# An expert chosen in the last mixer block becomes job 0: its weights load over the mixer's weights, and its token list is made ahead of the job table

## What is computed

```python
h    = rms_norm(x, norm_mix)
proj = h @ w_in + b_in                       # gates and u of a short convolution | q, k, v
x    = x + concat(rms_norm(y_conv), rms_norm(y_attn)) @ w_out + b_out
h2   = rms_norm(x, norm_ffn)
logits = h2 @ w_router + b_router            # 32 experts
top_vals, top_idx = lax.top_k(logits, 4);  gates = softmax(top_vals)
# for each expert e, over the tokens that picked it:
hid = h2[toks] @ w1[e] + b1[e]               # w1[e] 1024 x 2048
y   = clamped_swiglu(hid) @ w2[e] + b2[e]    # w2[e] 1024 x 1024
x[toks] += gate * y
```

## Time and profile before

| | us |
|---|---|
| median of 3 runs | 1974.45 |
| lowest, highest | 1973.93, 1977.43 |
| span of the profiled execution | 1973.8 |
| mixer, start to the barrier's release | 0 to 461.95 |
| setup of the experts, to the first piece of job 0 | 461.95 to 490.11 |
| jobs, to the end | 490.11 to 1973.8 |
| PE busy | 1912.5 (97%) |
| DVE busy | 1302.9 (66%) |

### The profile page before, as it was taken

The page is one execution under the profiler, slowest core; times in us unless marked ns, Lnnn a source line. Parts: engine busy times, 40 slices in busy tenths (PEclk is TensorE's granted clock), DMA queues, the critical chain, the costliest instruction groups (busy, mean ns, idle before and its releaser), DMA issues.

```text
span 1973.8 us, 33290 instructions
## 1 busy us (share of the span) xinstructions
PE 1912.5 (97%) x12224; PEld 1390.5 (70%) x12224; DVE 1302.9 (66%) x3759; ACT 411.4 (21%) x910; POOL 238.3 (12%) x317
## 2 busy tenths in 40 slices
PE   7999999997999999999999999999899999999996
PEld 5677777774999999999999999833334444444442
DVE  2787778764376777776666666634537766777665
ACT  1233332222121122222222222222212100001100
POOL 1212222221010011111111111110100000000000
PEclk9999999998999999999999999999999999999998
DMA  9411100004966787788888989999999999999992
GB/s 310 113 43 43 43 22 31 32 33 150 340 208 218 248 271 258 245 282 282 283 287 294 307 295 310 312 377 373 358 379 384 358 361 354 368 369 367 361 360 71
DMA packets 207682, 498.39 MB, mean 253 GB/s; under 512 B 7716, under 2 KB 14928, under 8 KB 200080
## 3 DMA queue, kind: packets, MB, share of 16 engines
q1 hardware_dynamic: 194016, 449.43, 63.2%
q0 software_dynamic: 11312, 39.85, 8.2%
q10 hardware_dynamic: 2304, 8.39, 1.0%
HBM read 470.24 MB, written 27.41 MB: 252 GB/s over the span
## 4 chain that ended last, share of the span: by engine, by line
PE 39%; issue 35%; POOL 1%; DVE 1%; DMA 0%; POOLq 0%; ACT 0%; DVEq 0%; ACTq 0%
PE ps_unit L1886 38%; POOL x_got L1378 1%; DMA x_got<-h_rows,idx_next 0%; PE ps_list L1858 0%; POOL carrier L1374 0%; POOL out_dram L1435 0%; POOLq L1096 0%; DVE match L1562 0%; POOL out_dram L1390 0%; DVE reached L1610 0%; POOLq L1426 0%; POOLq L1265 0%; DVE xT L1684 0%; ACT xT L1466 0%; POOLq L1413 0%
## 5 line engine op out<-in xcount | busy, mean ns | idle before, releaser
L1886 PE MATMUL ps_unit<-xT,w_slot 128*128 128x136 f32 (+6 forms) x3840 | 521.5, 298 | 1.5 <-DVE xT L1684 1.5
L1886 PEld LDWEIGHTS ps_unit<-xT,w_slot 128*128 128x128 f32 x3840 | 516.6, 196 | 1.9 <-issue 1.9
L1916 PE MATMUL ps_unit<-w_slot,xT 128*128 128x512 f32 x704 | 306.7, 594 | 1.2 <-DVE xT L1279 1.2
L1279 DVE STREAM_TRANSPOSE xT<-x_got 32x256 f32<-32x256 f32 x644 | 280.5, 436 | 30.5 <-DMA x_got<-h_rows,idx_next 22.0
L1886 PE MATMUL ps_unit<-act_T,w_slot 128*128 128x136 f32 (+6 forms) x1920 | 261.6, 298 | 0.1
L1886 PEld LDWEIGHTS ps_unit<-act_T,w_slot 128*128 128x128 f32 x1920 | 257.9, 190 | 2.2 <-DVE act_T L1659 1.5
L1916 PEld LDWEIGHTS ps_unit<-w_slot,xT 128*128 128x128 f32 x704 | 132.8, 190 | 164.3 <-issue 164.3
L1675 DVE STREAM_TRANSPOSE y_rows<-yT 32x256 f32<-32x256 f32 x372 | 162.1, 436 | 55.0 <-ACT yT L1481 50.1
L928 PE MATMUL ps_c<-hT,w_in_sb 128*128 128x128 f32 x1536 | 182.0, 278 | 5.5 <-DMA w_in_sb<-in_w_in_dram 5.5
L928 PEld LDWEIGHTS ps_c<-hT,w_in_sb 128*128 128x128 f32 x1536 | 177.2, 194 | 10.7 <-DMA w_in_sb<-in_w_in_dram 6.3
L1374 POOL TENSOR_TENSOR carrier<-carrier 128x1 f32<-128x1 f32 x64 | 15.8, 247 | 1320.4 <-issue 610.7
(11 more groups left out here) (294 smaller groups left out, 1835.6 us busy)
## 6 DMA issues: line engine op xcount, KB each, us to landing
w_slot<-in_w_dram SPq DMA_DIRECT2D x192, 2048.0 KB, 11.1
b_row<-in_b_dram SPq DMA_DIRECT2D x11, 1024.0 KB, 12.9
w_in_sb<-in_w_in_dram SPq DMA_DIRECT2D x6, 1024.0 KB, 12.0
b_row<-in_b_dram SPq DMA_DIRECT2D x11, 512.0 KB, 15.1
x_in<-in_x_dram SPq DMA_DIRECT2D x8, 512.0 KB, 3.5
x_res<-in_x_dram SPq DMA_DIRECT2D x8, 512.0 KB, 4.8
out_dram<-x ACTq DMA_DIRECT2D x8, 512.0 KB, 5.3
h_rows<-h ACTq DMA_DIRECT2D x8, 512.0 KB, 3.3
```

The lines of the kernel that those rows point to most:

```text
L1279: last = nc.vector.transpose(out[c * Q:(c + 1) * Q, :, tokens], rows.rearrange("p (k c j) -> p k c j", c=P // Q, j=Q)[:, :, c, :])
L1886: last = pe.matmul(ps_unit[p % RING][:, u, 0:n], w, moving[:, k, 0:n], start=(k == 0), stop=(k == KD - 1))
L1916: last = pe.matmul(ps_hid[c], xT[:, k, 0:P], w_slot[:, c, k, :], start=(k == 0), stop=(k == KD - 1))
```

## The change

1. In the last block PE sums the picks of the first seven blocks (`ps_tally`), and DVE takes the expert with the most (`choose_first`): a copy, a max, its index and two casts into `first_e` and `first_i`. This stands between two conv steps of DVE and its wait for the attention scores.
2. The expert slots are no longer memory of their own: `w_slot` lies over the mixer's weights in one tensor `w_store`. In the last block SP loads job 0's first-layer weights after `conv_done[3]` and its second-layer weights after `attn_mixed`. POOL loads the bias rows after `attn_mixed`, into what was left of `w_store` and into `x_in`.
3. In the setup DVE first works out the places of the chosen expert's tokens alone, then its size class, and POOL splits that expert's gates. PE lists the tokens before it does anything for the table. `hold_clock(5)` at the start and eight `hold_clock` matmuls ahead of the jobs go; `hold_clock(6)` comes in ahead of `first_rows`.
4. DVE's work on the table follows after the list of job 0 is read. A new term `leads` of the order key puts the chosen expert first.
5. PE runs job 0 from a body of its own, one for each of the 12 sizes, found by a chain of compares. In it, the keys are spread after piece 0, the fields after piece 1, and the list of job 1 is made after piece 4 instead of 2. PE reads the counts of jobs only after job 0, and its loops start at job 1.
6. The copies `iota_b` and two fifths of `entry` move from ACT in the setup to DVE ahead of the first block.

```diff
+            sp.wait_ge(first_chosen, 1)
+            e = sp.value_load(first_i[0:1, 0:1], min_val=0, max_val=NE - 1)
+            wait(sp, conv_done[CC - 1], NB - 1)
+            for i in range(W1_LOADS):
+                load_pieces(sp, w_slot, w1, w2, w_loaded, i, e)
+            wait(sp, attn_mixed, NB - 1)
+            for i in range(W1_LOADS, LOADS):
+                load_pieces(sp, w_slot, w1, w2, w_loaded, i, e)
...
+                if not more:
+                    wait(pool, x_normed, t)
+                    wait(pool, attn_mixed, t)
+                    pool.dma_start(b1_rows[:, 0:D], b1[0, :, 0:D]).then_inc(pool_moved.sem, 16)
+                    pool.dma_start(b1_rows[:, D:2 * D], b1[0, :, D:2 * D]).then_inc(rows_moved.sem, 16)
+                    pool.dma_start(b2_rows, b2[0]).then_inc(pool_moved.sem, 16)
...
+            def choose_first():
+
+                dve.wait_ge(tallied, 1)
+                fstep.did(nc.vector.tensor_copy(tally[:], ps_tally))
+                dve.wait_ge(fstep.sem, fstep.n)
+                fstep.did(nc.vector.max(tally_top[:], tally[:]))
+                dve.wait_ge(fstep.sem, fstep.n)
+                fstep.did(nc.vector.max_index(tally_i[:], tally_top[:], tally[:]))
+                dve.wait_ge(fstep.sem, fstep.n)
+                fstep.did(nc.vector.tensor_copy(first_e[:], tally_i[:, 0:1]))
+                dve.wait_ge(fstep.sem, fstep.n)
+                nc.vector.tensor_copy(first_i[:], first_e[0:1, :]).then_inc(first_chosen, 1)
...
+                if not more:
+                    wait(pe, added_up, NB - 2)
+                    pe.matmul(ps_tally, ones_b[:], before[:, NB - 1, :], start=True, stop=True).then_inc(tallied, 1)
...
-            pool.dma_start(y_rows[0:NE, 0, :], b1[0, :, 0:D]).then_inc(pool_moved.sem, 16)
-            pool.dma_start(y_rows[0:NE, 1, :], b1[0, :, D:2 * D]).then_inc(rows_moved.sem, 16)
-            pool.dma_start(b2_rows[0:NE, :], b2[0]).then_inc(pool_moved.sem, 16)
+            e0 = pool.value_load(first_i[0:1, 0:1], min_val=0, max_val=NE - 1)
+            first_gate = gates[:, :, bass.ds(e0, 1)].rearrange("p b o -> p (b o)")
+            gate_step(nc.gpsimd.tensor_copy(entry[:, :, 2], first_gate))
...
+            e0 = dve.value_load(first_i[0:1, 0:1], min_val=0, max_val=NE - 1)
+            ranks = ps_list[:, 0:NB * NE].rearrange("p (b e) -> p b e", b=NB)
+            dve.wait_ge(ranked, 1)
+            v.tensor_copy(first_count[:], ps_list[:, bass.ds(e0 + NB * NE, 1)])
...
+            then_wait(v.tensor_scalar(leads[:], first[:], 0.0, -LEAD, ALU.is_equal, ALU.mult))
+            then_wait(v.scalar_tensor_tensor(out=leads[:], in0=ended[:], scalar=first_e[:], in1=leads[:], op0=ALU.is_equal,
+                                             op1=ALU.mult))
+            then_wait(v.tensor_tensor(past[:], past[:], leads[:], ALU.add))
...
+            def first_job(v):
+
+                for p in range(PIECES):
+                    piece(0, p, SIZES[v])
+                    if p == 0:
+                        spread_keys()
+                    if p == 1:
+                        spread_fields()
+                    if p == 4:
+                        list_tokens(1, ps_list[:, 0:10])
...
-            hold_clock(5)
...
-            list_tokens(0)
+            pe.wait_ge(first_gates.sem, first_gates.n)
+            list_tokens(0, ps_first)
             pe.wait_ge(units_cleared, RING)
             biases()
+            pe.wait_ge(first_sized, 1)
+            first_class = pe.value_load(first_size_i[0:1, 0:1], min_val=0, max_val=last_size)
+            hold_clock(6, ps_flat[RING - 1])
+            first_rows()
+            pe.wait_ge(biases_read, 3)
+            choice = nc.cur_bb
+            for v in range(last_size, 0, -1):
+                pe.br_eq(first_class, v, on_true=f"first_job_{v}", on_false=f"first_job_below_{v}")
+                with nc.body(f"first_job_{v}", valid_engines=[mybir.EngineType.PE]):
+                    first_job(v)
+                    pe.br("past_first_job")
+                nc.switch_bb(f"first_job_below_{v}")
+            first_job(0)
             pe.wait_ge(table_ready, TABLES)
             words = []
             for i in range(WORDS):
-                hold_clock(2)
                 words.append(pe.value_load(ends[0:1, COLUMNS + i:COLUMNS + i + 1], min_val=0,
```

More of the change, by code:

```diff
@@ L56 @@
 LOADS = PIECES // 2
+LEAD = 2048.0
 PW = 256
@@ L1059, in _, with experts @@
             hold_clock(3, cst)
-def experts(nc, h2_rows, out_rows, w1, b1, w2, b2, cst, tri_b, ones_b, picked, gates, before, token, limits, marks):
+def experts(nc, h2_rows, out_rows, w1, b1, w2, b2, cst, tri_b, ones_b, picked, gates, before, token, limits, marks, iota_b,
+            entry, w_slot, w_loaded, first_e, first_i, b1_rows, b2_rows, pool_moved, rows_moved):
     ident = cst[:, C_ID:C_ID + P]
@@ L1196, in experts @@
         xT_ready = event("xT_ready")
-        w_loaded = [event(f"w_loaded{i}", 16) for i in range(LOADS)]
         unit_done = [event(f"unit_done{p}", 1, 1) for p in range(PIECES)]
@@ L1466, in _ @@
                 nc.scalar.copy(xT[:, 2 * i:2 * i + 2, :], ps_x[i][:]).then_inc(xT_read, 1)
+            act.wait_ge(parts_left[1], 1)
+            nc.scalar.copy(gate_parts[:, :, 2, :], gates[:]).then_inc(parts_cast[2], 1)
             def wide_job(q):
@@ L1500, in _ @@
             wide, slim_jobs, narrow_jobs, full = job_counts(act)
-            with act.If(wide > 0):
-                with act.Fori(0, wide) as q:
-                    wide_job(q)
+            with act.Fori(0, wide) as q:
+                wide_job(q)
             def slim_sigmoid(s, t):
@@ L1853, in _, with list_tokens @@
         def _(pe):
-            def list_tokens(t):
+            def list_tokens(t, lists):
                 wait(pe, matched, t)
@@ L1857, in list_tokens @@
                     for b in range(NB):
-                        last = pe.matmul(ps_list[:, 5 * h:5 * h + 5], match[:, b, h * P:(h + 1) * P], entry[:, b, :],
+                        last = pe.matmul(lists[:, 5 * h:5 * h + 5], match[:, b, h * P:(h + 1) * P], entry[:, b, :],
                                          start=(b == 0), stop=(b == NB - 1))
@@ L2109, in _ @@
             with pe.If(slim_jobs > 0):
-                with pe.If(wide < 1):
-                    first_rows()
                 with pe.Fori(0, slim_jobs) as s:
@@ L2115, in _ @@
             with pe.If(narrow_jobs > 0):
-                with pe.If(full < 1):
-                    first_rows()
                 with pe.Fori(0, narrow_jobs) as t:
```

215 lines of the change are left out of this document (127 added, 88 removed).

## The result

| | before | after |
|---|---|---|
| median, us | 1974.82 (4 runs) | 2009.47 (4 runs) |
| lowest, highest | 1973.93, 1977.43 | 2007.73, 2010.75 |
| profiled span, us | 1973.8 | 2008.0 |
| PE busy | 1912.5 (97%) | 1913.6 (95%) |

The ratio is 1.0173, with a 95% interval of 1.0162 to 1.0185. The forecast was 1968.3, range 1963.5 to 1975.5.

The account below looks back on a forecast made before the run. PE, busy for 97% of the span, was taken to set the pace, so starting jobs earlier ends them earlier. 9.4 - 0.7 - 0.5 - 1.1 - 1.0 = 6.1 us of gain gave a median of 1968.3, range 1963.5 to 1975.5.

Parts of the forecast that it names:

- the rival: Jumps around job 0 wait for code that is not there: slower, 1976 to 1986 us; chance 0.14.
- own sign of being wrong: Wrong if PE idles over 3 us with issue as the reason ahead of job 0 or job 1.
- C: From the barrier to job 0: job 0 begins at 480.7, a gain of 9.4 us, ends 11.1 and 6.0.
- E: Between jobs 0 and 1: register loads, register operations and two jumps lose 1.0 us, between 0 and 2.7.
- The two change places: Job order: expert 18, size 192, becomes job 0 and expert 31, size 208, job 1; cost zero.
- The rival's size: Each unhinted jump costs 1.1 to 2.6 us, from a code packet's time and the fastest landing.
- its two places: Ahead of job 0 and between jobs 0 and 1: stalls and half clock, 18.6 us together at 2.6 a jump.
- A: Choosing the expert in the last block: DVE's added steps lose 0.7 us, ends 0.2 and 0.9.
- B: The mixer's end: h2's store, SP's loads or POOL's transfers delay the barrier by 0.5 us, ends 0 and 3.
- the cover: At the mixer's end: h2's store landed about 457.1, 3.5 us early; beside weights it lands at 459.7 to 462.8.
- D: Inside job 0: table matmuls for keys and fields, 0.66 and 0.48 us, lose 1.1 us.
- No clip held PE in job 0: DVE's table work beside job 0 costs nothing, with 12 us left; a clip holding PE would show it wrong.

Follow-up runs that it names:

- experiment 1: The changed kernel with size 192 compared first in the chain ahead of job 0; 1991.59 us, 1.0083 to the kernel before.
- experiment 5: The changed kernel with a single job 0 body (size 192), no compares or exit jump, and no loop of size 256; 1981.93 us.
- experiment 3: The kernel before without the branch hints on jumps over sizes that have no jobs; 1998.48 us, 1.0115.
- experiment 2: The changed kernel with expert 31 (size 208) as job 0 whatever the tally says; 1991.89 us, 1.0081 to the kernel before.
- experiment 4: The changed kernel with a single job 0 body (size 192), no compares ahead and no jump out; 1997.05 us, 1.0104 to the kernel before.
- experiment 7: The changed kernel with one job 0 body and loops only for sizes that have jobs, so no far jumps; 1967.81 us, 0.9959 to the kernel before.
- experiment 6: The changed kernel with the eleven compares side by side and job 0's twelve bodies behind them; 1992.28 us, 1.0085 to the kernel before.
- experiment 11: The general version built on the changed kernel, without hints in the size loops except the last loop's; 1978.46 us, 1.0021 to the kernel before.
- experiment 9: The changed kernel with compares side by side, announced exits, hinted jumps to the next size with jobs, and 256's loop last; 1975.32 us, 1.0004.
- experiment 10: The changed kernel with each job 0 body announcing its jump out at its start; 2002.59 us, 1.0139 to the kernel before.

## Why the prediction was wrong

**The mechanism was among the rivals**, with a chance of 0.14 and 1976 to 1986 us. Three steps failed, and a size. The forecast's own sign of being wrong, over 3 us of idle time with "issue" as the reason ahead of either job, came true at both.

1. **C: "Then one turn of four tiles, 1.09, and the same 2.64 us from the second turn's start to the first piece".** This path to job 0 has no term for the three jumps over bodies, though the rival names them. The turns began at 478.27 and the first piece at 493.77, 12.7 us later than in experiment 1, which has no such jump, and the piece took 2.8 us longer. That is 15.5 of the 34 us, the largest part.
2. **E: "two jumps ... Between 0 and 2.7 I take 1.0."** The loads were sized right, 1.46 us with nothing to cover them (experiment 5). The two jumps were given nothing, because job 1 had followed job 0 without a gap though a size was jumped over the earlier trace rows. That row shows an announced jump. Experiment 3 takes its announcement away and the gap appears. The row was no evidence for the new jumps, and the text said so itself: "no row shows an unhinted far one".
3. **"The two change places, so no matmul is added or saved: zero."** True of matmuls, but size 192 lost its only loop job, so PE goes from 208 to 176 over three sizes, two of them unannounced. 11.45 us of stall and 2.0 of half clock. Neither the forecast nor the rival had this place; in experiment 2, which leaves 192 its job, the stall is 2.69 us.
4. **The rival's size: 1.1 to 2.6 us a jump**, from one code packet and one fast landing. Behind job 0 a jump took 4.7 to 5.7 us (experiments 2, 4, 5). Ahead of job 0 PE's program waits for the gather, which lands at about 476.9 (471.93 + 4.8 to 5.1); if PE's sequencer went on from there, the three up to 493.77 make 5.6 each, an estimate. A packet's time on the queue is not the time of a jump. With 5 us a jump, the rival's own arithmetic for its two places gives some 30 us in place of its 18.6 at most.

**What was right**, by the same steps:
- **A**, 0.7 forecast: DVE's last step on the gates starts at 460.80 for 460.25, 0.55 us.
- **B**, 0.5: the release is at 462.72 for 461.98, 0.74 with A's part, so 0.2. SP's six issues end at 455.7 in place of 457 forecast. h2's last store, issued at 455.02, lands in 6.2 us instead of 2.6, at 461.2, level with DVE's last result at 461.17, so the cover was used up.
- **C up to the turns**, and its end where no jump stands: job 0 at 481.05 in experiment 1, whose release was 0.43 later than before, so 480.6 on the forecast's own scale for 480.7. In part that is luck. The list came at 466.83 and landing took 4.8 us, as stated. But the gathers started at 470.55 and 471.93, 1.2 us after the forecast, the second outside the stated 469 to 471: POOL began to clear the rows at 467.84 in place of 466.27. They landed before PE wanted them all the same. `hold_clock` took 8.20 us for 6.9 (8.00 in experiment 1, 6.80 in experiment 7, within the stated ends), and from the turns' start to the first piece it was 3.3 us in experiment 1 in place of 3.7. In experiment 7 the release came 1.5 us late, at 463.46, and the short `hold_clock` made up for it: job 0 at 480.94.
- **D**, 1.1: keys and fields took 0.49 and 0.16, so 0.65.
- No clip held PE in job 0.

The forecast's sum was 1968.3, and experiment 7, with the same work and without far jumps, measured 1967.8. The gain it shows is 6.8 to 7.7 us for the forecast's 6.1; by the steps above it would be 9.5 - 0.55 - 0.2 - 0.65 - 1.46 = 6.6. That A, B and D came out cheaper by 0.9 us together and E dearer by 0.5 is why the total is so close. What the forecast left out were seven unannounced jumps.

**The Trainium skill** (Runtime: NRT & Kernel Launch, "Instruction fetch mechanics") says that a taken branch whose target is outside the prefetched pages must wait for a fetch. The runs agree in kind, with 4.7 to 5.7 us for each of the jumps behind job 0. That compares next to each other cost nothing that shows while three jumps over bodies do (experiment 6) fits that rule too. That the stall is a fetch is inferred: from this, from the 16 KB packets in it and from the hints. No run measured the fetch by itself.

## What stays open

Single unannounced jumps took 1.7, 7.2 and 8.0 us in experiment 3, 5.7 in experiment 4, 2.6 and 3.9 in experiment 11, and nothing that shows ahead of job 0 in experiments 2 and 6. Announced ones took nothing in the kernel before and from 168 to 152 in experiment 9, but 2.69 us in experiment 2, and the announced exit of experiment 10 gave back only 2.4 us. Moving code by other edits changed some of these (15.01 against 11.45 in experiment 4, 10.99 against 13.60 in experiment 10). Where a target lies against the packets' borders could do that; it was not tried. Whether a general kernel can have experiment 7's 7 us, with the jump from 208 to 176 announced too, is open.

## To carry to other kernels

Draw the jumps of an engine's program before and after a change, with the amount of code each one passes, for the inputs that are run, and mark which are announced: where several follow each other, each unannounced one costs about as much as a whole piece of a job here (5.5 us), and the clock behind the stall 1.7 to 2.8 us more. Put compares side by side with the bodies behind them, and check which loops a reordering of work leaves empty. When the only row for a cost shows the favourable kind (announced, hidden, short), it bounds nothing for the other kind: give that rival its chance by the code, not by the row.

## What the runs showed of the hardware

- One unannounced jump over bodies of over 200 matmuls each: 4.7 to 5.7 us where several follow each other (7.5 once), 1.7 to 8.0 alone, and nothing that shows where a gather and copies run beside it. Announced ones took nothing in the kernel before, and took away 3.9 us of idle time and 2.7 us of half clock at one place (experiments 9 and 11). In the first stall from 484 to 488 no engine works, and 5 packets of 16 KB arrive in 14 us.
- The first stall costs more than its length: PEclk is 0.50 in it, and the next 32 records took 8.29 us for 5.47.
- A 512 KB gather landed in 4.8 us with nothing beside it (8.8 beside weight loads); a 512 KB store took 6.2 us beside weight loads, 2.6 without.
- Five register loads from on-chip tables, with their register work and nothing over them, held PE for 1.46 us.
